# A hybrid decoder layer: the whole value rows of the second tile spread among the partial ones, and its late adds in halves

## The reference

```
expert_idx = (16 best of 128 x 128 pairs of keys, per head and token)   # first key * 128 + second key
gate = softmax(best scores)
act  = gelu(expert_u[expert_idx] . x)
out  = sum over the 128 chosen experts of gate * act * expert_v[expert_idx]
return rms_norm(h + out, final_norm)
```

## Time and profile before

| | us |
|---|---|
| median of 3 runs | 2016.02 (2013.01 to 2017.6) |
| profiled execution, span | 2008.7 |
| PE busy | 1770.1 (88%) |
| DVE busy | 1368.9 (68%) |
| POOL busy | 1040.7 (52%) |
| late adds, L1464, mean of one over 2048 columns | 2.35 |

### The profile page before, as it was taken

The page is one execution under the profiler, slowest core; times in us unless marked ns, Lnnn a source line. Parts: engine busy times, 40 slices in busy tenths (PEclk is TensorE's granted clock), DMA queues, the critical chain, the costliest instruction groups (busy, mean ns, idle before and its releaser), DMA issues.

```text
span 2008.7 us, 18796 instructions
## 1 busy us (share of the span) xinstructions
PE 1770.1 (88%) x6283; PEld 1122.4 (56%) x6283; DVE 1368.9 (68%) x2191; ACT 574.5 (29%) x1037; POOL 1040.7 (52%) x643
## 2 busy tenths in 40 slices
PE   7999999999999999875565578898887899999996
PEld 6888888888888898622222233344333554444442
DVE  5463453233334338999889887787888888888956
ACT  5445464345543520210111132233313740000001
POOL 5443343444332413575555565465555668877732
PEclk9999999999999999887778899999998899999999
DMA  8986454665555679999999999999999999999997
GB/s 211 241 177 148 142 189 152 192 196 180 169 164 173 204 263 403 384 411 420 418 419 417 402 420 419 414 413 414 403 415 391 401 369 408 409 414 386 409 421 308
DMA packets 157641, 647.28 MB, mean 322 GB/s; under 512 B 25894, under 2 KB 31086, under 8 KB 95598
## 3 DMA queue, kind: packets, MB, share of 16 engines
q0 software_dynamic: 73728, 450.98, 55.2%
q1 hardware_dynamic: 83824, 195.16, 30.9%
HBM read 729.91 MB, written 2.10 MB: 364 GB/s over the span
## 4 chain that ended last, share of the span: by engine, by line
PE 52%; DMA 18%; DVE 13%; issue 9%; POOL 7%; POOLq 0%; ACT 0%; DVEq 0%; SPq 0%; ACTq 0%
DMA u_ring<-in_peer_u_dram,idx 10%; PE acc L1583 10%; PE acc L1585 10%; PE acc L1584 10%; PE misc L1967 8%; PE acc L1967 8%; DMA u_high<-in_peer_u_dram,idx 3%; DVE u_ring L1425 3%; DMA u_mid<-in_peer_u_dram,idx 3%; DVE u_ring L1423 3%; POOL u_ring L595 3%; POOL v_high L602 1%; POOL u_mid L595 1%; DVE u_mid L1425 1%; DVE u_mid L1423 1%
## 5 line engine op out<-in xcount | busy, mean ns | idle before, releaser
L553 POOL TENSOR_TENSOR w_lo<-raw,w_hi 128x1024 fp32r<-128x1024 f32 x112 | 276.3, 2467 | 421.0 <-ACT w_hi L677 420.7
L1583 PE MATMUL acc<-w_hi,t_hi 128*128 128x512 f32 x896 | 355.0, 396 | 0.0
L1585 PE MATMUL acc<-w_hi,t_lo 128*128 128x512 f32 x896 | 349.3, 390 | 0.0
L1584 PE MATMUL acc<-w_lo,t_hi 128*128 128x512 f32 x896 | 348.9, 389 | 0.0
L1025 DVE TENSOR_TENSOR w_lo<-raw,w_hi 128x1024 fp32r<-128x1024 f32 x112 | 158.4, 1415 | 265.7 <-ACT w_hi L677 265.6
L595 POOL DMA_INDIRECT u_ring<-in_peer_u_dram,idx x160 | 210.2, 1314 | 249.0 <-DVE dots L1425 195.1
L677 ACT ACTIVATE w_hi<-raw 128x1024 fp32r<-128x1024 f32 x224 | 237.0, 1059 | 330.8 <-PE acc L1585 281.1
L1932 PE MATMUL misc<-v_high,diag 128*128 128x512 f32 x368 | 203.7, 705 | 87.0 <-DMA v_high<-in_peer_v_dram,idx 84.2
L1932 PE MATMUL misc<-v_low,diag 128*128 128x512 f32 x368 | 191.7, 670 | 79.1 <-DMA v_low<-in_peer_v_dram,idx 79.1
L1423 DVE CUSTOM_DVE_ANT_0 u_ring<-u_ring,hn 128x1024 f32<-128x1024 f32 x160 | 195.8, 1224 | 72.5 <-DMA u_ring<-in_peer_u_dram,idx 65.8
L1425 DVE CUSTOM_DVE_ANT_0 u_ring<-u_ring,hn 128x1024 f32<-128x1024 f32 x160 | 195.3, 1221 | 0.0
(11 more groups left out here) (286 smaller groups left out, 2433.4 us busy)
## 6 DMA issues: line engine op xcount, KB each, us to landing
u_ring<-in_peer_v_dram SPq DMA_DIRECT2D x48, 1024.0 KB, 8.9
raw<-in_w_in_dram SPq DMA_DIRECT2D x64, 512.0 KB, 7.0
raw<-in_xattn_wk_dram SPq DMA_DIRECT2D x32, 512.0 KB, 4.6
raw<-in_xattn_wv_dram SPq DMA_DIRECT2D x32, 512.0 KB, 3.9
raw<-in_w_out_dram SPq DMA_DIRECT2D x32, 512.0 KB, 4.7
raw<-in_xattn_wq_dram SPq DMA_DIRECT2D x32, 512.0 KB, 4.9
raw<-in_xattn_wo_dram SPq DMA_DIRECT2D x32, 512.0 KB, 4.8
praw<-in_peer_wq_dram SPq DMA_DIRECT2D x24, 512.0 KB, 8.6
```

Of the source, the lines that this page charges most:

```text
L553: nc.gpsimd.tensor_tensor(w_lo[:, j % RING, :, :], raw[:, j % RING, :, :], w_hi[:, j % RING, :, :].bitcast(F32), ALU.subtract).then_inc(lo ...
L1583: nc.tensor.matmul(o, xh, w_hi[:, s, kk, :], start=first, stop=False)
L1584: nc.tensor.matmul(o, xh, w_lo[:, s, kk, :], start=False, stop=False)
L1585: ins = nc.tensor.matmul(o, xl, w_hi[:, s, kk, :], start=False, stop=last)
```

## The change

The 32 whole rows get places among the 96 partial ones: late_row(m) says which of the second tile's 128 gathers is the m-th late row. The first four are partial, then about every fourth is whole (m = 4, 7, 11, 15, ... 108, 112, 116, 120, 124), and the last three are partial. Slots, the PE rows and the order of all else stay. Each late add of DVE becomes two instructions, of the left and the right 1024 columns, each with a semaphore of its own for the sum before it (v_left and v_added). In the last rows before add_last the left one covers columns 512 to 1023.

```diff
+        SPREAD = 4
+        PARTIAL = TOP * (PH - WHOLE)
+        def whole_before(m):
+            return max(0, min(TILE0 - PARTIAL, ((m - SPREAD) * (TILE0 - PARTIAL) + TILE0 - SPREAD - 1) // (TILE0 - SPREAD)))
+        def late_row(m):
+            w = whole_before(m)
+            return PARTIAL + w if whole_before(m + 1) > w else m - w
...
-                gather_v(TILE0 + m, v_slot(slot), late_landed[slot])
+                gather_v(TILE0 + late_row(m), v_slot(slot), late_landed[slot])
...
             def add_values(m):
                 dve.wait_ge(late_landed[late_slot(m)], 16 * late_use(m))
+                row, c, k = v_slot(late_slot(m)), PH + late_row(m) // TOP, late_row(m) % TOP
+                before = y_sum if m else h
+                at = 0 if m < SHARED else CW
+                if m:
+                    dve.wait_ge(v_left, added_before(m))
+                nc.vector.scalar_tensor_tensor(y_sum[:, 1, at:D // 2], row[:, at:D // 2], low_wts[:, c, k:k + 1],
+                                               before[:, 1, at:D // 2], ALU.mult, ALU.add).then_inc(v_left, 1)
                 if m:
                     dve.wait_ge(v_added, added_before(m))
-                at = 0 if m < SHARED else CW
-                nc.vector.scalar_tensor_tensor(y_sum[:, 1, at:], v_slot(late_slot(m))[:, at:], low_wts[:, PH + m // TOP, m % TOP:m % TOP + 1],
-                                               (y_sum if m else h)[:, 1, at:], ALU.mult, ALU.add).then_inc(v_added, 1)
+                nc.vector.scalar_tensor_tensor(y_sum[:, 1, D // 2:], row[:, D // 2:], low_wts[:, c, k:k + 1],
+                                               before[:, 1, D // 2:], ALU.mult, ALU.add).then_inc(v_added, 1)
...
                 if m == 3:
                     weights(GROUPS - 1)
+                    dve.wait_ge(wts_ready, GROUPS)
```

More of the change, by code:

```diff
@@ L263, in hybrid_layer @@
         dve_step, act_step, pool_step, passed = sem("dve_step"), sem("act_step"), sem("pool_step"), sem("passed")
-        x_squared, table_ready, zero_ready, v_added, y_scaled = sem("x_squared"), sem("table_ready"), sem("zero_ready"), sem("v_added"), sem("y_scaled")
+        x_squared, table_ready, zero_ready, v_left, v_added, y_scaled = sem("x_squared"), sem("table_ready"), sem("zero_ready"), sem("v_left"), sem("v_added"), sem("y_scaled")
         block = ctx.enter_context(nc.Block())
@@ L399, in hybrid_layer @@
         FINISH = LATE + 6
+        SPREAD = 4
[5 more added lines that the diff above has]
+            return PARTIAL + w if whole_before(m + 1) > w else m - w
+        assert sorted(map(late_row, range(TILE0))) == list(range(TILE0))
         def by_pe(m):
@@ L893, in late_diagonal @@
                 nc.scalar.activation(diag[:, n % 4, :], ident[:, :], ACT.Copy,
-                                     scale=low_wts[:, PH + m // TOP, m % TOP:m % TOP + 1]).then_inc(diag_ready, 1)
+                                     scale=low_wts[:, PH + late_row(m) // TOP, late_row(m) % TOP:late_row(m) % TOP + 1]).then_inc(diag_ready, 1)
             def weights_T(b):
@@ L1479, in add_last @@
                     cols = slice(i * CW, (i + 1) * CW)
-                    nc.vector.scalar_tensor_tensor(y_sum[:, 1, cols], v_slot(late_slot(m))[:, cols], low_wts[:, PH + m // TOP, m % TOP:m % TOP + 1],
+                    nc.vector.scalar_tensor_tensor(y_sum[:, 1, cols], v_slot(late_slot(m))[:, cols], low_wts[:, PH + late_row(m) // TOP, late_row(m) % TOP:late_row(m) % TOP + 1],
                                                    y_sum[:, 1, cols], ALU.mult, ALU.add).then_inc(y_added, 1)
```

## The result

The changed kernel takes 2026.09 us (median of 4 runs, 2024.42 to 2026.88), the kernel before 2014.97 us beside it (2013.01 to 2017.60, 4 runs): ratio 1.0050, 95% interval 1.0038 to 1.0062. It is slower by 11.1 us, 0.55%. The forecast was slower, 2020.5 us, +4.5. A measure that leaves out what differs ahead of the late rows is the time from the first late add to the end of the last three pieces: 362.1 us before (1638.38 to 2000.49) and 376.6 after (1640.00 to 2016.59).

The account below looks back on a forecast made before the run. The DMA was taken to set the late rows' pace. More DVE work after 1963.4 us (+5.1) less 0.6 gained before gave +4.5 us: span 2013.2, plus 7.3, is 2020.5 us; range 2011 to 2026 us.

Parts of the forecast that it names:

- The halves: Late adds on DVE: two overlapping halves take 2.41 us per row instead of 2.455, a gain of 0.045 us per add.
- the order, up to 1961 us: Late rows until the last dense tile is in: same DMA bytes and rate, fewer rows; DVE keeps up without a lead.
- a row or two further back: Bound for rows landed when the dense tiles end: fewer than counted, +2.4 us per row, up to +9 us.
- What was to be gained before: DMA holes before the late rows and around 1850 us: partly filled, counted -0.6 us; at most 5.2 us of DMA.
- The bytes decide and DVE fits: Rival for the tail: DMA bytes set the end and DVE's adds fit beside them; 2016 us, within 2; chance 0.22.
- The holes close and the tail stays open: Rival: deeper queues keep all 16 DMA engines fed, around 1850 us too, and DVE's lead holds; about 2011 us; chance 0.16.
- POOL is shut out: Rival for rows 119 to 127: halves without a gap delay POOL's gathers, 5 to 10 us on top, 2026 us; chance 0.10.
- the likeliest case: After the dense tiles, DVE's remaining adds set the end: 2020.5 us, 2016 to 2025 us; chance 0.52.

Follow-up runs that it names:

- even sets: Every partial row fetches a fixed 80 of 128 rows, five of each eight neighbouring partitions: old order 2011.31 us, changed kernel 2013.31 us.
- the last two edits: Kernel before with the first tile's stores held until the last row has landed, 2014.07 us; the same with its sums one add earlier, 2014.85 us.

## Why the prediction was right, and where its size was off

**The mechanism.** The forecast said that the order leaves more rows for the time after the dense tiles, and that DVE, not the DMA, then sets the end. Both hold: no landing is waited for after 1963.20, the DMA falls to 0.86 and 304 GB/s, and half of each add left out takes 6.7 us off the changed kernel's median.

**The halves.** Forecast 2.41 us per row, measured 2 x 1.195 = 2.39, against 2.455. Without any overlap it would have been 2.57 (2 x 1.285): 0.09 us of each half is hidden behind the other when nothing is waited for. The rule of the Trainium skill that two instructions pay a fixed latency twice ("VectorE: DVE Perf Modes", section on the TRN2 errata) agrees with the durations, where two halves come to 0.22 us more than a whole add (2 x 1.285 - 2.35), and not with the pitch. All the same the halves are worth nothing here, ratio 1.0001 by themselves, since the DMA sets the pace of the old order.

**The step that failed in size** is *the order, up to 1961 us*: "the DMA does the same bytes by 1961 us, at the same rate, but in fewer rows", from which row 109 and twelve full adds followed. The bytes are right to 0.5 MB, but the rows were taken from the mean, as if bytes that had been moved were rows that had landed. Row 109 landed at 1969.8, not before 1963.4. Rows 105 on were left: 16 adds, 4 x 2.39 = 9.6 us more. With even sets, where the mean is nearer the truth, the traces of the two orders lie 5.2 us apart, where the forecast had 5.1; that they agree so closely may be chance. The forecast's own bound for a frontier "a row or two further back, because few of the partial rows' bytes fall on the engines that lag" named the cause and gave it half its size: it is not the exception but the case.

**The sum again**, from 1963.20: 16 adds 38.2; first sums 2.4; gain 1.26; scaling 2.0; take_sums after 1.59 of waiting for PE 3.5; two adds 3.9; the pieces 2.1: 53.4 us, to 2016.59. Beside the four adds the one new term is the wait for PE, which the forecast had done 1 us before DVE, and which was done 1.6 us after it. The matrix for row 122 came as forecast, 1.85 us after the scaling began (2000.35 to 2002.20) and ready 0.4 us later. But PE had then been idle for 4.42 us, the granted clock stands at 0.50, and the eight matmuls of the row took 6.04 us where the forecast had 3.43:

```profile
2002.73 6.04 PE L1962 MATMUL acc<-late_h,diag 128*128 128x512 f32 x8 [4.42 <-ACT diag L907]
```

```profile
2001.00:2005.00 4.00, 2.27 (x3) 1.18 (x4) 3.96 (x5) 2.32 (x5) 0.00 (x0) 0.50 0.56 226
```

Before, that row took 3.67 us, 1.24 us after the work ahead of it. At 3.60 us, as rows 116 and 119 took, PE would have been done at 2006.3, ahead of DVE's last full add (2007.2), and DVE would not have waited (an estimate). The lower clock of that row is what the forecast had not counted.

**What was to be gained before** (-0.6 us; by its own terms a quarter of a row, 0.45 of 1.8 us, and not the third that it names) did not come. The hole before the late rows stayed; the one around 1850 us closed, and its bytes went into rows that were not complete.

**The other rivals.** *The bytes decide and DVE fits* falls with the count of adds. *The holes close and the tail stays open* has one of its two signs, 418 GB/s around 1850 us, and not the other, row 109 before 1958 us; nothing was gained by it. *POOL is shut out* falls: from 1696 to 1840 us a gather lasts 1.29 us in the mean (59.22 us, 46 of them) and not 2.12 as before (114.55, 54), though single ones still take 2.1, and GpSimd waits for slots that DVE frees. The section of "SBUF — State Buffer" in the Trainium skill on who interferes with whom fits the lockstep of before; with a boundary every 1.2 us no cost of it shows here (ratio 1.0001 with halves alone).

**The base, and luck.** The forecast added 7.3 us to its span, as what surrounds the program. In the changed kernel's execution that is 1.9 us (2026.21 - 2024.3). The other 5.4 us are an execution of before that was ahead before its late rows began: its first late add stands at 1638.38 us, and at 1642.48, 1643.39 and 1643.87 in the traces of the halves alone and of the last two edits, which keep the old order. From there to the last piece all four take 362.1 to 362.7 us. So 8 adds are left at 1963 us in that execution, and 9 with halves alone, whose span is 2014.4. The span was forecast at 2013.2 us and came at 2024.3, 11.1 us later; the time was missed by only 5.6 us because the 5.4 us of an early execution had been added to it. That 2026.09 us lies at the upper end of the range is luck as well: the likeliest case ended at 2025, and the 2026 of the range came from *POOL is shut out*.

## What to carry to other kernels

A gather with skipped rows has to be forecast by when its rows are complete, not by the mean bytes: count the rows that are out and incomplete (issued rows less bytes moved over the bytes of a row), and ask whether the skipped ones are evenly spread over the partitions. Uneven rows belong where their consumer has slack and something even follows them, so that the lag ends as bytes; at the end of the list the lag ends as work of the consumer. A full DMA line in a stretch says that bytes are moved, not that rows are finished. And a profiled execution is one of many: count a stretch from an event that begins it, not from the start of the span.

## What had not been expected of the hardware

A skew of 10% over the partitions, at equal bytes and equal row sizes, cost 14.4 us of 2013.31 (2027.73) by medians, and 12.4 us in the traces from the first late add on (376.0 against 363.6). How the partitions are shared out among the 16 DMA engines is not in these views; that the spread over the partitions matters is.

TensorE's late rows also ran slower behind a gap, and one of these gaps was on the path (row 122, above). In the changed kernel PE waited 6.99 us for row 113, and its eight matmuls then took 6.38 us instead of the 3.60 of the next eight; the granted clock of the stretch is 0.50, the lower of the two levels, 1.2 of 2.4 GHz. That row was not waited for; row 122 was. PE's timeline and the stretch:

```profile
1974.77 6.38 PE L1962 MATMUL acc<-late_h,diag 128*128 128x512 f32 x8 [6.99 <-DMA late_h<-in_peer_v_dram,idx]
1980.98 3.60 PE L1988 MATMUL acc<-u_ring,wT 128*128 128x512 f32 x8
```

```profile
1972.00:1978.00 6.00, 3.23 (x4) 1.52 (x5) 6.00 (x6) 0.00 (x0) 3.09 (x3) 0.50 0.88 335
```
